# Where four heads' scores and a step's values stand in a projection loop with stick-breaking attention woven in

## The reference

```python
def stick_breaking(q, k, v, q_pos, k_pos):
    z = jnp.einsum('bqhd,bkhd->bhqk', q, k).astype(jnp.float32) * (D_HEAD ** -0.5)
    causal = k_pos[None, :] < q_pos[:, None]
    log_keep = jnp.where(causal, jax.nn.log_sigmoid(-z), 0.0)
    log_after = lax.cumsum(log_keep, axis=3, reverse=True) - log_keep
    a = jnp.where(causal, jnp.exp(jax.nn.log_sigmoid(z) + log_after), 0.0)
    return jnp.einsum('bhqk,bkhd->bqhd', a.astype(v.dtype), v)
```

## Time and profile before

| | us |
|---|---|
| median of 3 runs | 2450.25 (2448.75 to 2451.13) |
| profiled execution | 2450.47 |
| its span | 2448.70 |
| PE busy | 2270.8 (93%) |
| PEld busy | 1753.7 (72%) |
| DVE busy | 941.7 (38%) |
| ACT busy | 856.8 (35%) |
| POOL busy | 506.9 (21%) |

### The profile page before, as it was taken

The page is one execution under the profiler, slowest core; times in us unless marked ns, Lnnn a source line. Parts: engine busy times, 40 slices in busy tenths (PEclk is TensorE's granted clock), DMA queues, the critical chain, the costliest instruction groups (busy, mean ns, idle before and its releaser), DMA issues. The chain is left out here.

```text
span 2448.7 us, 46127 instructions
## 1 busy us (share of the span) xinstructions
PE 2270.8 (93%) x16622; PEld 1753.7 (72%) x16625; DVE 941.7 (38%) x1657; ACT 856.8 (35%) x1913; POOL 506.9 (21%) x405
## 2 busy tenths in 40 slices
PE   6999999999999999988999998888799867999996
PEld 4887777777777777775999998555455544777885
DVE  5111111212111111125488885533233348876123
ACT  4001332223222232212344443355455466662100
POOL 5433222222222222223100000000000000444332
PEclk7999999999999999999999999899899976999998
DMA  4755676767676767568566664899999976002423
GB/s 148 216 176 200 236 257 212 264 224 261 228 242 230 265 225 265 191 165 208 177 195 194 196 196 136 276 373 382 278 381 380 313 230 201 1 1 95 128 79 120
DMA packets 321699, 523.15 MB, mean 214 GB/s; under 512 B 36981, under 2 KB 128518, under 8 KB 319638
## 3 DMA queue, kind: packets, MB, share of 16 engines
q1 hardware_dynamic: 300642, 487.56, 60.1%
q10 hardware_dynamic: 16416, 23.13, 2.9%
q0 software_dynamic: 4416, 9.52, 1.2%
HBM read 497.83 MB, written 44.00 MB: 221 GB/s over the span
## 5 line engine op out<-in xcount | busy, mean ns | idle before, releaser
L549 POOL TENSOR_TENSOR proj_w_lo<-kept_region,proj_w_hi 128x1024 fp32r<-128x1024 f32 (+1 forms) x120 | 282.5, 2355 | 720.8 <-DVE proj_w_hi L800 720.8
L580 PE MATMUL proj_acc<-proj_w_hi,h_hi 128*128 128x512 f32 (+1 forms) x952 | 389.8, 409 | 0.0
L582 PE MATMUL proj_acc<-proj_w_lo,h_hi 128*128 128x512 f32 (+1 forms) x952 | 368.9, 388 | 0.0
L581 PE MATMUL proj_acc<-proj_w_hi,h_lo 128*128 128x512 f32 (+1 forms) x952 | 368.2, 387 | 0.0
L752 ACT COPY proj_kT<-proj_tp 128x512 f32<-128x512 f32 x256 | 150.3, 587 | 402.8 <-PE proj_tp L641 348.2
L800 DVE CAST proj_w_hi<-kept_region 128x1024 fp32r<-128x1024 f32 (+1 forms) x120 | 86.9, 726 | 382.8 <-PE proj_acc L584 380.1
L580 PEld LDWEIGHTS proj_acc<-proj_w_hi,h_hi 128*128 128x128 f32 x952 | 179.1, 188 | 60.3 <-issue 31.7
L582 PEld LDWEIGHTS proj_acc<-proj_w_lo,h_hi 128*128 128x128 f32 x952 | 178.7, 188 | 37.5
L581 PEld LDWEIGHTS proj_acc<-proj_w_hi,h_lo 128*128 128x128 f32 x952 | 179.6, 189 | 27.6
L1206 ACT COPY cmp_xT<-cmp_tp 128x512 f32<-128x512 f32 x260 | 139.0, 588 | 159.7 <-PE cmp_tp L1119 159.7
L641 PE MATMUL proj_tp<-kept_consts,kept_region 128*128 128x128 f32 x1024 | 153.7, 272 | 0.1
(11 more groups left out here) (459 smaller groups left out, 3640.3 us busy)
## 6 DMA issues: line engine op xcount, KB each, us to landing
kept_region<-in_cache_sb_kv_dram SPq DMA_DIRECT2D x256, 256.0 KB, 4.9
kept_second<-in_cache_sb_kv_dram SPq DMA_DIRECT2D x256, 256.0 KB
kept_second<-in_cache_nsa_kv_dram SPq DMA_DIRECT2D x512, 128.0 KB, 2.4
kept_region<-in_w_in_dram SPq DMA_DIRECT2D x112, 512.0 KB, 6.1
kept_region<-in_cache_nsa_kv_dram SPq DMA_DIRECT2D x128, 256.0 KB, 5.0
kept_region<-in_cache_dsa_kv_dram SPq DMA_DIRECT2D x128, 256.0 KB, 4.7
kept_second<-in_cache_nsa_kv_dram SPq DMA_DIRECT2D x64, 256.0 KB, 4.9
kept_rows<-in_cache_nsa_kv_dram SPq DMA_DIRECT2D x64, 256.0 KB, 5.2
```

Of the source, the lines that this page charges most:

```text
L549: pool.tensor_tensor(w_lo[p % SPLIT][:, :, here], w[p % RAW][:, :, here], w_hi[p % SPLIT][:, :, here], ALU.subtract).then_inc(lo_made, 1)
L580: pe.matmul(to, h_hi[:, kk, r], hi[:, k], start=first, stop=False)
L581: pe.matmul(to, h_lo[:, kk, r], hi[:, k], start=False, stop=False)
L582: last = pe.matmul(to, h_hi[:, kk, r], lo[:, k], start=False, stop=final)
```

## The change

Three things are changed. The scores of all four heads are issued at place 9, where the last two stood, and the values of the step before right behind them, also at place 9 (before: at place 4, behind the first two heads). For this kT keeps four heads, and the copy of a turned key waits for the score of the same head one step earlier. The value pages of the next step are loaded at place 12 in place of 8. The room for the larger kT comes from the four small tiles of the new keys, which now lie inside kT and kept.oTs. As VALUES_AT is part of LAST, the last turning moves back by five places.

```diff
--- before.py
+++ after.py
@@ -372,13 +372,14 @@
         k_rows = kept.region[:, 4096:8192].rearrange("p (b m c) -> p b m c", b=PER, m=PPS)
         v_rows = kept.second[:].rearrange("p (b m c) -> p b m c", b=PER, m=PPS)
         v_new = kept.second[0:NT].rearrange("p (b c) -> p b c", c=CH)
-        kT = s.sb("kT", [P, 2, PER, KEYS_S])
+        kT = s.sb("kT", [P, HEADS, PER, KEYS_S])
         soft = [s.sb(f"soft{i}", [P, KEYS_S]) for i in range(2)]
         prob = [s.sb(f"prob{i}", [P, KEYS_S]) for i in range(2)]
         pT = [s.sb(f"pT{i}", [P, PPS, P]) for i in range(2)]
         got = s.sb("got", [P, GROUPS, CH])
-        soft_new, log_new = s.sb("soft_new", [P, GROUPS, NT]), s.sb("log_new", [P, GROUPS, NT])
-        prob_new, pT_new = s.sb("prob_new", [P, GROUPS, P]), s.sb("pT_new", [NT, GROUPS, P])
+        soft_new = kept.oTs[:, 0, 0:GROUPS * NT].rearrange("p (g t) -> p g t", t=NT)
+        log_new = kT[:, HEADS - 1, 2, 0:GROUPS * NT].rearrange("p (g t) -> p g t", t=NT)
+        prob_new, pT_new = (kT[0:rows, HEADS - 1, i, :].rearrange("p (g r) -> p g r", r=P) for i, rows in enumerate((P, NT)))
         tp = s.ps("tp", [P, CH])
         logits = s.ps("logits", [P, CH])
         sc, qp = logits[:, 0:KEYS_S], logits[:, KEYS_S:CH].rearrange("p (m r) -> p m r", r=P)
@@ -407,8 +408,7 @@
 
         TURN_Q, TURN_K, NEW = BLOCKS + 4, 2 * BLOCKS + 4, 3 * BLOCKS + 2
         FIRST, EACH = 3 * BLOCKS + 16, 13
-        PROBS_AT, VALUES_AT, NEXT_VALUES_AT, SOFTEN_AT, EXP_AT = 1, 4, 8, 9, 11
-        SCORES_AT = (4, SOFTEN_AT)
+        PROBS_AT, SOFTEN_AT, VALUES_AT, EXP_AT, NEXT_VALUES_AT = 1, 9, 9, 11, 12
         LAST = FIRST + STEPS * EACH + VALUES_AT + 2
         assert LAST < chunks * BLOCKS
         index_at = [FIRST + STEPS * EACH + x for x in (0, 10, 20, 30)]
@@ -427,9 +427,9 @@
             if step < STEPS:
                 if i < 2 * HEADS:
                     fill(step, i)
-                if i in SCORES_AT:
-                    for h in range(2):
-                        score(step, 2 * SCORES_AT.index(i) + h)
+                if i == SOFTEN_AT:
+                    for h in range(HEADS):
+                        score(step, h)
                 if i == SOFTEN_AT:
                     soften(step)
                 if i == EXP_AT:
@@ -650,7 +650,7 @@
                         pe.wait_ge(new_got, GROUPS)
                 pe.wait_ge(kT_copied, step * 2 * HEADS + 2 * h + 2)
                 for r in range(PER):
-                    last = pe.matmul(sc[r * RISE:(r + 1) * RISE, :], q_sb[:, g * PER + r, h, :], kT[:, h % 2, r, :],
+                    last = pe.matmul(sc[r * RISE:(r + 1) * RISE, :], q_sb[:, g * PER + r, h, :], kT[:, h, r, :],
                                      start=(h == 0), stop=(h == HEADS - 1), skip_group_check=True, tile_position=(0, r * RISE))
                 last.then_inc(scored, 1)
 
@@ -746,10 +746,10 @@
             def fill(step, i):
                 h, pair = divmod(i, 2)
                 act.wait_ge(k_turned, step * 2 * HEADS + i + 1)
-                if step * HEADS + h >= 2:
-
-                    act.wait_ge(scored, step * HEADS + h - 1)
-                act.copy(kT[:, h % 2, 2 * pair:2 * pair + 2, :], tp[:].rearrange("p (b k) -> p b k", b=2)).then_inc(kT_copied, 1)
+                if step:
+
+                    act.wait_ge(scored, (step - 1) * HEADS + h + 1)
+                act.copy(kT[:, h, 2 * pair:2 * pair + 2, :], tp[:].rearrange("p (b k) -> p b k", b=2)).then_inc(kT_copied, 1)
 
             def soften(step):
                 to = soft[step % 2][:]
```

## The result

| | before | after |
|---|---|---|
| median | 2449.5 us (4 runs, 2446.8 to 2451.13) | 2433.72 us (4 runs, 2430.4 to 2434.27) |
| profiled execution | 2450.47 us | 2434.27 us |
| its span | 2448.7 us | 2432.2 us |

The ratio is 0.9935 with an interval of 0.9923 to 0.9947: faster by 13.0 to 18.9 us.

A forecast was written before the change was run, and what follows sets the result against it. TensorE, issuing without a gap in the projection, was taken as the bound. From 2450.47 us, 10.6 for passages and 1.8 for late values gave 2438.07, against the median 2437.85; forecast 2437.8 us, range 2434.3 to 2442.0.

The forecast's parts named there:

- The bound: Input projection: TensorE is busy without a gap, so time is what it issues plus changes between kinds of matmul.
- The sum of what is moved: Places 4 and 9: one passage between array forms goes per step, 0.33 us in 32 steps, 10.6 us saved.
- Rival 4: Passage cost sits in neighbouring transposes or products in both forms; only 3 to 6 us saved, 2444 to 2447; chance 4%.
- Feeding the burst: Merged group at place 9: scores keep their pace, 0.054 us each, two more heads taking 0.87 us.
- Rival 3: Merged group's burst is fed too slowly, 0.12 us per added pair of heads; 3.9 us lost, 2441.7; chance 3%.
- The page loads: Value pages issued at place 12 get 23 us of room in place of 15; late values vanish, saving 1.8 us.
- The keys, costed at nothing: Key loads keep places 6 and 7 and get 2.7 us more before first use; taken at no gain or loss.
- Rival 2: Keys come late, transposes at place 0 wait; 1 us late per step gives 2469; chance 4%.
- Moved waits, at nothing: Projection: shifted waits on VectorE, SP and ScalarE cost nothing; TensorE gets no new semaphore waits.
- Rival 1: Another chain holds the projection; TensorE's saved time becomes a wait for low halves of weights, about 2450; chance 5%.
- What follows the projection starts behind its barrier ... so the gain reaches the end whole: Stages behind the projection: they start behind its barrier, so its gain reaches the total unchanged.

The follow-up runs named there:

- v9_s4_9: Against the changed kernel: two heads' scores moved back to place 4, two stay at place 9 with the values behind; 2444.1 us, ratio 0.9979.
- v4_s9: Against the changed kernel: values alone at place 4, their pages loaded at place 8, all four heads' scores at place 9; 2448.6 us, ratio 1.0001.

## Why the prediction was right and where it failed

**The bound** was read rightly: TensorE issues without a gap, and its sum of starts sets the projection.

**The sum of what is moved** was right: 10.6 us forecast; a merged group measured 4.24 us as forecast, transposes 0.66 for 0.67, and a passage 0.31, 0.34 and 0.35 us from three pairs of variants, where the rounded rows had given 0.33. The 32 passages that the change itself takes out, v9_s4_9 against after, gave 9.9 us. Rival 4 (only part of the passage is saved) is out with these figures.

**Feeding the burst**: 32 scores took 616.25 - 614.50 = 1.75 us up to the values; 0.89 + 0.87 = 1.76 was forecast. Rival 3 is out: the row shows 0.055 us each. The Trainium skill, page "TensorE: Matmul & The Clock Gate", section "Wait — 56ns, not 53.3ns?", states about 62 ns per matmul with hardware decode off; the trace shows less per matmul, so that bound does not hold here.

**The page loads**: the late values vanished as forecast. The term was taken at 1.8 us; v9_s4_9, which moves the values and keeps 65 groups, is 1.8 us shorter than v4_s9 and 2.4 to 3.2 shorter than the traces of before. The step was right and its size at or a little under what was measured. The prediction counted the three waits of 300 to 1000 us and left out a fourth of 0.3 us ahead of them; what the rest would be, no run shows. The keys, costed at nothing, caused no wait of note. Rival 2 (late keys) is out.

**Moved waits, at nothing**: confirmed. TensorE shows no new wait that lengthens the projection. Low halves of weights were waited for 5.0 us in six by the weight loads, 0.8 at most each, at places where 0.8 us stand for the values' end in any case (before, the same gaps were booked as "issue"), and the projection got shorter by the whole sum, 12.3 and 13.0 us where 12.4 were forecast. Rival 1 is out.

**"What follows the projection starts behind its barrier ... so the gain reaches the end whole"**: this is the step that failed. The gain reached the end with 3 to 4 us on top, which the sum had at nothing. The prediction looked for what the shorter projection might collide with inside the projection, and took everything behind it as a rigid block that slides forward. It was not rigid: in the trace of before, a load came 4.7 us late at the end of slc, and that wait was not read, because it lay 650 us behind the projection. With the change the waits of the streams for key blocks fell from 6.0 and 4.1 us to 1.2 and 0.4. Their size (streams 414.1 and 413.1 against 409.5 and 409.6) is as large as the whole distance of 4.1 us from the forecast to the measurement. The range failed for the same reason: it took its allowance from three runs that lay within 2.4 us, and 94 runs of the same kernel spread over 15. It was also uneven: 2.8 us were allowed below the sum of the terms and 1.7 above, which is less than the "somewhat more" than 2.4 that the text promises. That the measured median missed the range by only 0.6 us says little; the term at fault is 3 to 4 us.

**What stays open**: why loads of slc come late in both traces of before and not in those of after. Shown is that the loads are late, that the streams are long where they are, that an eighth less to move was not enough to bring them in time, and that with more compute per step none is late. Whether the moment at which the streams begin decides it, or the order of loads in the projection, or both, is not shown. If the late loads were removed in before, the two kernels should differ by the projection alone, 12 to 13 us; in no experiment were the totals tight enough to show that.

## What to carry to other kernels

Where small column-tiled matmuls are woven between full-array ones, count the passages between the forms, not the matmuls: stand everything that is tiled together, here for 0.31 to 0.35 us per passage, and buffer what that needs. The price is invisible in busy time; read it from start to start in the timeline, where it can be summed to a few hundredths of a microsecond per step before anything is built. And when a change slides the later stages, read the waits of those stages too: a load that is late is part of the sum, in either direction, and a range wants more than three runs. A trace is one execution: compare its time with the median before a small wait in it is taken for the kernel's.

## What the runs showed of the hardware

Column tiles between full-array products cost a passage, 0.31 to 0.35 us there and back. Transposes between them show none: 0.66 us for four and a product, start to start, leaves 0.11 for each transpose beside the 0.23 of a product. Column tiles overlap: 32 scores of 256 columns took 1.75 us, 0.055 each, half of what a transpose of 128 columns took. Moving an eighth less did not bring the late loads in time, while in the traces with more compute in each step none was late. And executions of one unchanged kernel, each on one core, spread over 15 us in 94 runs on four chips, while the changed kernel stayed within 4.2 us in eight.
